# Turning the cached keys on VectorE during the FFNs, with a copy of them in HBM

## The reference

```
x = x + 0.5 * post1(SwiGLU_1(pre1(x)))      # 1024 -> 2816 -> 1024
z = pre_m(x) @ w_in                         # 2832 columns: GLA, stick-breaking attention, convolution
x = x + post_m(concat(groups) @ w_out)
x = x + 0.5 * post2(SwiGLU_2(pre2(x)))
```

```
past_k = cache_sb_k[l][page_table].reshape(DB, past_len, SB_HEADS, SB_DIM)
z = einsum('bqhd,bkhd->bhqk', q, k) * d**-0.5 + bias_h
A[t,s] = sigmoid(z_ts) * prod_{s<j<t} (1 - sigmoid(z_tj));   out = A @ v
```

## Time and profile before

| | |
|---|---|
| time, median of 3 runs | 1406.8 us (1406.1 to 1408.73) |
| span of the profiled execution | 1407.3 us |
| TensorE busy | 1391.1 us, 99% |
| VectorE busy | 899.6 us, 64% |
| ScalarE busy | 734.5 us, 52% |
| GpSimd busy | 182.6 us, 13% |
| HBM read, written | 242.10 MB, 5.53 MB |
| mean granted TensorE clock | 0.998 of full speed |

### The profile page before, as it was taken

The page is one execution under the profiler, slowest core; times in us unless marked ns, Lnnn a source line. Parts: engine busy times, 40 slices in busy tenths (PEclk is TensorE's granted clock), DMA queues, the critical chain, the costliest instruction groups (busy, mean ns, idle before and its releaser), DMA issues.

```text
span 1407.3 us, 26950 instructions
## 1 busy us (share of the span) xinstructions
PE 1391.1 (99%) x10551; PEld 1321.4 (94%) x10551; DVE 899.6 (64%) x1508; ACT 734.5 (52%) x1210; POOL 182.6 (13%) x333
## 2 busy tenths in 40 slices
PE   7999999999999999999999999999999999999998
PEld 6999999988878999999999999999888799999998
DVE  5666544669995876663367665346899858756542
ACT  4544434489766554443365444346887665444441
POOL 1020000323262110000000000021433510000000
PEclk9999999999999999999999999999999999999999
DMA  9575455577799595545545555564868895555541
GB/s 247 150 210 150 141 147 153 156 203 230 210 310 265 145 255 150 150 139 152 155 127 149 151 149 144 152 175 141 252 206 242 287 255 154 151 149 149 148 139 50
DMA packets 391554, 249.41 MB, mean 177 GB/s; under 512 B 16513, under 2 KB 379638, under 8 KB 391428
## 3 DMA queue, kind: packets, MB, share of 16 engines
q1 hardware_dynamic: 375602, 204.94, 51.2%
q0 software_dynamic: 15520, 42.62, 9.7%
q10 hardware_dynamic: 306, 0.13, 0.0%
HBM read 242.10 MB, written 5.53 MB: 176 GB/s over the span
## 4 chain that ended last, share of the span: by engine, by line
PE 94%; DVE 2%; ACT 1%; DMA 1%; issue 1%; SPq 0%; POOLq 0%; POOL 0%; DVEq 0%; ACTq 0%
PE bank L596 25%; PE bank L598 24%; PE bank L597 24%; PE bank L862 3%; PE bank L973 2%; PE bank L877 2%; PE bank L632 2%; PE bank L636 2%; PE bank L633 2%; PE bank L1050 1%; DMA raw<-in_ffn_w_gate 1%; PE bank L827 1%; PE bank L954 1%; PE bank L1168 1%; PE bank L1090 1%
## 5 line engine op out<-in xcount | busy, mean ns | idle before, releaser
L1602 DVE TENSOR_TENSOR w_l<-raw,w_h 128x1024 fp32r<-128x1024 f32 (+1 forms) x332 | 395.4, 1196 | 295.4 <-ACT w_h L1224 295.1
L596 PE MATMUL bank<-hh,w_h 128*128 128x320 f32 x1632 | 512.9, 314 | 0.0
L598 PE MATMUL bank<-hh,w_l 128*128 128x320 f32 x1632 | 504.4, 309 | 0.0
L597 PE MATMUL bank<-hl,w_h 128*128 128x320 f32 x1632 | 504.3, 309 | 0.0
L1224 ACT ACTIVATE w_h<-raw 128x1024 fp32r<-128x1024 f32 (+1 forms) x332 | 332.3, 1030 | 141.4 <-DMA raw<-in_ffn_w_down 101.4
L596 PEld LDWEIGHTS bank<-hh,w_h 128*128 128x128 f32 x1632 | 306.4, 188 | 11.8 <-issue 8.6
L597 PEld LDWEIGHTS bank<-hl,w_h 128*128 128x128 f32 x1632 | 306.5, 188 | 0.6
L598 PEld LDWEIGHTS bank<-hh,w_l 128*128 128x128 f32 x1632 | 306.4, 188 | 0.0
L596 PE MATMUL bank<-guh,w_h 128*128 128x320 f32 x704 | 217.7, 309 | 0.0
L598 PE MATMUL bank<-guh,w_l 128*128 128x320 f32 x704 | 217.4, 309 | 0.0
L597 PE MATMUL bank<-gul,w_h 128*128 128x320 f32 x704 | 217.4, 309 | 0.0
(11 more groups left out here) (297 smaller groups left out, 1604.9 us busy)
## 6 DMA issues: line engine op xcount, KB each, us to landing
raw<-in_ffn_w_gate SPq DMA_DIRECT2D x88, 512.0 KB, 4.0
raw<-in_ffn_w_up SPq DMA_DIRECT2D x88, 512.0 KB, 3.9
raw<-in_ffn_w_down SPq DMA_DIRECT2D x64, 448.0 KB, 3.8
raw<-in_w_in SPq DMA_DIRECT2D x44, 512.0 KB, 4.0
raw<-in_ffn_w_down SPq DMA_DIRECT2D x32, 512.0 KB, 4.0
kpg<-in_cache_sb_k SPq DMA_DIRECT2D x112, 128.0 KB, 3.3
kpg<-in_cache_sb_k POOLq DMA_DIRECT2D x112, 128.0 KB, 2.7
raw<-in_w_out SPq DMA_DIRECT2D x16, 512.0 KB, 6.9
```

The source lines that it names most:

```text
L596: pe.matmul(out, w_h[:, slot, k, :], rhs_h[:, k0 + k, :], start=first, stop=False)
L597: pe.matmul(out, w_h[:, slot, k, :], rhs_l[:, k0 + k, :], start=False, stop=False)
L598: last = pe.matmul(out, w_l[:, slot, k, :], rhs_h[:, k0 + k, :], start=False, stop=end)
L1602: V(dve.tensor_tensor(w_l[:, slot, 0:n, :], raw[:, slot, 0:n, :], w_h[:, slot, 0:n, :].bitcast(F32), ALU.subtract), sm["w_lo"])
```

## The change

- TensorE turns no keys any more, and ScalarE copies none. `kpz`, `kpg`, `turn_keys`, `turn_keys_early` and `copy_keys` are gone.
- A staged unit is the 4 pages of one batch in one step, 32 of them per layer. GpSimd loads the rows into `kn_` with 32 partitions for each quarter (`load_rows`, four DMAs of 128 KB), VectorE turns all 32x32 blocks by one instruction of 128x1024 into `kx_`, and GpSimd stores them to a new tensor `turned_keys` in HBM by four DMAs in pieces of 512 B (`store_turned`). Both buffers are double.
- VectorE's turns stand at fixed places in the FFNs: all 32 units of layer 0 in its first FFN (one a pair from the third pair on, then two for each of six output tiles); the 32 of layer 1 in the two FFNs between the mixers, 16 each.
- In the mixer SyncE alone loads a whole step from `turned_keys` (4 DMAs of 512 KB, 4 KB in one piece for each partition) to `kT`, double buffered by step. A score call covers a whole step, 512 columns, at the `m` of `SCORES_AT`, alternating between banks 4 and 2.
- GpSimd does its other work of the mixer (state loads, clearing buffers) after all stores of that layer's keys have landed (`all_stored`). The values of steps 0 and 1 are loaded when the score calls 6 and 7 are done.
- Some start-up semaphores are merged.

```diff
+SCORES_AT = {9: 0, 10: 1, 12: 2, 13: 3, 15: 4, 17: 5, 19: 6, 21: 7}
+SCORE_BANK = (4, 2)
...
+    turned_keys = nc.dram_tensor("turned_keys", [L, ITS, G, P, 2, 4, P], F32, kind="Internal").ap()
...
@@ SyncE
-                def keys(h):
...
-                        for j in range(2):
-                            sp_.dma_start(heads(kpg[l][:, h % 2, b, j, :]), page(sp_, ids[4 * b + 2 * (h % 2) + j], ins["cache_sb_k"], l)).then_inc(sm[f"ks_loaded{h % 2}"], 16)
+                def keys(it):
+
+                    for b in range(G):
+                        if it < 2:
                             sp_.wait_ge(sm["w_used"], U + U_IN + 4)
                         else:
+                            sp_.wait_ge(*at("kt_used", it - 1))
+                        sp_.wait_ge(sm[f"kx_stored{b % 2}"], 64 * (l * UNITS_K // 2 + 2 * it + b // 2 + 1))
+                        sp_.dma_start(kT[l][it % 2][:, b], turned_keys[l, it, b].rearrange("p a n s -> p a (n s)")).then_inc(sm[f"ks_loaded{it % 2}"], 16)
...
-                keys(2)
-                keys(3)
+                keys(0)
+                keys(1)
                 load_in(8)
                 load_in(9)
                 for m in range(7, 20):
                     load_in(m + 3)
-                    for h in range(4, 2 * ITS):
-                        if SLOT_OF[h - 2] == m:
-                            keys(h)
+                    for it in range(2, ITS):
+                        if SCORED[it - 2] == m:
+                            keys(it)
@@ GpSimd
+                def load_rows(i):
+
+                    g = l * UNITS_K + i
+                    if g >= 2:
+                        pool.wait_ge(sm["kx_turned"], g - 1)
+                    page_ids(pool, ids, i // G, (i % G,))
+                    for n in range(4):
+                        pool.dma_start(kn_[32 * n:32 * n + 32, g % 2], quarter(pool, ids[n], ins["cache_sb_k"], l)).then_inc(sm[f"kn_loaded{g % 2}"], 16)
+
+                def store_turned(i):
+
+                    g = l * UNITS_K + i
+                    pool.wait_ge(sm["kx_turned"], g + 1)
+                    for n in range(4):
+                        pool.dma_start(turned_keys[l, i // G, i % G, :, :, n, :].rearrange("(r p) a s -> p a r s", p=32),
+                                       kx_[32 * n:32 * n + 32, g % 2].rearrange("p (a r) s -> p a r s", a=2)).then_inc(sm[f"kx_stored{g % 2}"], 16)
...
                 else:
-                    pool.wait_ge(sm["w_used"], 16)
-                pool.wait_ge(sm["pages_loaded"], 32)
-                page_ids(pool, ids, 0, range(G))
-                for h in range(2):
-                    for b in range(G):
-                        for j in range(2):
-                            pool.dma_start(heads(kpz[:, h, b, j, :]), page(pool, ids[4 * b + 2 * h + j], ins["cache_sb_k"], l)).then_inc(sm["kz_loaded"], 16)
+                    pool.wait_ge(sm["w_used"], 8)
+                pool.wait_ge(sm["const_loaded"], 48)
+                load_rows(0)
+                load_rows(1)
+                for i in range(UNITS_K):
+                    store_turned(i)
+                    if i + 2 < UNITS_K:
+                        load_rows(i + 2)
+                all_stored(pool, l)
@@ TensorE
-                def turn_keys(h, batches):
...
+                def scores(it):
+
+                    pe.wait_ge(*at(f"ks_loaded{it % 2}", 64 * (it // 2 + 1)))
...
+                    if it >= 2:
+                        pe.wait_ge(*at("z_placed", it - 1))
+                    out = bank[SCORE_BANK[it % 2]]
                     for p_ in range(2):
                         for b in range(G):
                             c0 = (it // (PAGES // 4) * G + b) * 32
+                            last = pe.matmul(out[32 * b:32 * b + 32, :], qb[:, p_, c0:c0 + 32], kT[l][it % 2][:, b, p_, :],
                                              start=(p_ == 0), stop=(p_ == 1), skip_group_check=True)
@@ VectorE
+            def turn_keys(k2, units):
+
+                for _ in range(units):
+                    if staged[0] >= (1, 1.5, 2, 2)[k2] * UNITS_K:
+                        return
+                    g = staged[0]
+                    dve.wait_ge(sm[f"kn_loaded{g % 2}"], 64 * (g // 2 + 1))
+                    if g >= 2:
+                        dve.wait_ge(sm[f"kx_stored{g % 2}"], 64 * (g // 2))
+                    V(dve.transpose(kx_[:, g % 2].rearrange("p c (j s) -> p j c s", s=32), kn_[:, g % 2].rearrange("p j (c d) -> p j c d", d=32)), sm["kx_turned"])
+                    staged[0] += 1
...
                         V(dve.tensor_tensor(gul[:, 2 * i + t, :], gt[:, t, :], guh[:, 2 * i + t, :].bitcast(F32), ALU.subtract), sm["gu_lo"])
+                        if i and (k2 == 0 or t == 0):
+                            turn_keys(k2, 1)
...
                 for n in range(KD):
                     for m in range(3):
                         if 3 * n + m + LEAD < 3 * KD + 5:
                             lo(Ud + 3 * n + m + LEAD)
+                    if n < KD - 2:
+                        turn_keys(k2, 2 if k2 == 0 else 1)
```

More of the change, by code:

```diff
@@ L359, in page, with quarter, all_stored @@
         return cache[l:l + 1, bass.ds(eng.snap(reg, min_val=0, max_val=cache.shape[1] - 1), 1)].rearrange("l n p h d -> p (l n h) d")
+    def quarter(eng, reg, cache, l):
+        return cache[l:l + 1, bass.ds(eng.snap(reg, min_val=0, max_val=cache.shape[1] - 1), 1)].rearrange("l n (j p) h d -> p (l n j) (h d)", p=32)
+    def all_stored(eng, l):
+        for half in range(2):
+            eng.wait_ge(sm[f"kx_stored{half}"], 64 * (l + 1) * UNITS_K // 2)
     def heads(ap):
@@ L428, in values @@
                         for b in (0, 1):
[L429 to L432, removed]
+                            if it < 2:
+                                sp_.wait_ge(*at("kt_used", ITS - 1 + it))
                             else:
@@ L546, in store_rows @@
                     pool.dma_start(outs["sample_sb_" + name][l].rearrange("b t h d -> (b t) (h d)"), t[0:TS, 2, :]).then_inc(so, 16)
-                for h in range(2, 2 * ITS):
-                    keys(h)
-                    if h == 8:
+                for it in (4, 5, 6):
+                    if it == 4:
                         pool.wait_ge(*at("sk_placed", 2))
                         store_rows("k", skn)
-                    if h == 10:
+                    if it == 5:
                         pool.wait_ge(*at("cso_placed", 2))
@@ L1013, in _ @@
                         gate_rows(u, out, range(4))
-                    elif h == last_h:
+                    else:
                         unit(u, out, hh, hl, part=range(4))
-                    else:
-                        unit(u, out, hh, hl, part=range(3))
-                        turn_keys(h, (2, 3))
-                        unit(u, out, hh, hl, part=range(3, 5))
-                        turn_keys(last_h, (0, 1))
-                        unit(u, out, hh, hl, part=range(5, 6))
-                        scores(h)
-                        unit(u, out, hh, hl, part=range(6, 7))
-                    if last_h < 2 * ITS:
-                        turn_keys(last_h, (2, 3))
                     if m == 9:
@@ L1044, in _ @@
                     else:
-                        unit(u, out, hh, hl, part=range(4, KD) if h == last_h else range(7, KD))
+                        unit(u, out, hh, hl, part=range(4, KD))
                 def gla_outputs(pair):
@@ L1926, in _ @@
                         place_prompt(m - 13)
-                    for h in TURNS[m]:
-                        if h >= 2 and h % 2 == 0:
-                            log_weights(h // 2 - 1)
+                    if m in SCORES_AT:
+                        log_weights(SCORES_AT[m])
                     if m == NIN - 1:
```

186 lines of the change are left out of this document (51 added, 135 removed).

## The result

The changed kernel is slower: 1421.95 us (median of 4 runs, 1419.82 to 1423.58) against 1407.39 us, ratio 1.0102 with a 95% interval of 1.0087 to 1.0116. The forecast was 1410 us, a range of 1394 to 1428, and slower as the likeliest sign. Sign and range hold; the forecast is 12 us too small, and what follows is about those 12 us.

What follows compares the result with a forecast made beforehand. TensorE was busy 1391.1 of 1407.3 us, with VectorE nearly full too in the projection loop. A 15.6 us first-FFN loss minus a 12.6 us mixer gain gave +3.0 on the median 1406.8: about 1410 us, range 1394 to 1428.

Steps and rivals of the forecast that it cites:

- The 50.5 us: Two projection loops: TensorE's queue gets 50.5 us shorter, by 58 groups of eight key transposes at 0.87 us each.
- the upper bound: Projection loops: the gain is at most VectorE's idle time, 13.4 us in layer 0 and 11.3 in layer 1, together 24.7.
- the 12.6 taken: Mixers' gain: 4.9 us before layer 0's second log weights, 2.9 in layer 1, 4.8 in the long stretches after.
- Unit 9's split: Mixer's projection: keys ahead in SyncE's queue delay unit 9's weights, so its split starts near 287.6 us, not 283.81.
- the 1.6 us of first latency: Mixer, SyncE's queue: an estimated 1.6 us within the landing time of unit 9's weights, near 285.8 us.
- the rule that the prediction quotes: Mixer's key loads: starting DMAs from several engines saves only start time, so the single queue costs nothing; about 4 us more gain.
- The cycle where VectorE is behind: FFN gate loop: 5.58 us plus 1.15 for a transpose makes 6.73 us a pair, under TensorE's 7.04.
- Turn 19: Layer 0's first FFN: transpose 19 ends at 181.4 us, and GpSimd's work on the remaining units is counted from there.
- 11 U - 54.8: Layer 0's first FFN: loss in us, U being GpSimd's us per staged unit; 15.6 at U = 6.4.
- this sign of being wrong: Staging: the prediction is wrong if GpSimd's cost per unit is far from 6.4 us.
- The DMAs saturate: Rival, first FFN: U = 7.5 costs 27.7 us, net +15, 1422 us; chance 0.16.
- 149 + 217 GB/s wanted: First FFN's down projection: DMA rates wanted, set against 289 to 327 GB/s seen, as support for saturated DMAs.

Runs made afterwards that it cites:

- the taps: Changed kernel without six of the convolution's 31 taps, VectorE work in the projection loop: 1409.20 us; the kernel before without the same six: 1408.53 us.
- the other order in the queue: Changed kernel with SyncE issuing the loads of projection units 8 and 9 between the first and second four key loads, not behind both: 1425.31 us.

## Why the prediction held in sign and missed in size

**The gain.** TensorE's transposes left and VectorE became the bound: shown by the taps. The 50.5 us gave back 15.3, under the 24.7 of the upper bound and near the 12.6 taken. The steps can be followed in VectorE's log weights (line 1847 before, 1799 after). From the copy to the second of them: 57.1 us before (308.01 - 250.92), 52.55 after (330.36 - 277.81), 4.5 gained for 4.9 forecast; in layer 1 55.05 and 52.5, 2.5 for 2.9. From there to the last of them: 86.1 us before (394.11 - 308.01 in layer 0), 83.7 after (414.09 - 330.36), the same in layer 1, 2.4 gained for 2.4 forecast. The forecast ended there. The remaining 0.9 and 2.6 us were gained behind the loop, where it had nothing.

```profile
330.36 0.68 DVE L1799 SCALAR_TENSOR_TENSOR t__108<-z__107,t__108 128x512 f32<-128x512 f32 x1
...
414.09 0.68 DVE L1799 SCALAR_TENSOR_TENSOR t__108<-z__107,t__108 128x512 f32<-128x512 f32 x1
```

**The single queue.** Unit 9's split was forecast 3.8 us late and came 3.7 late (36.6 us after the copy; 32.9 before), though the 1.6 us of first latency in that sum had no row behind them. But the forecast booked this as lost gain, and with the other order in the queue nearly none of it came back: the next wait was as long. The event was right and its price wrong. That order was tried within one queue; two queues were not, so the rule that the prediction quotes from the Trainium skill, "DMA: Bandwidth & Descriptors", section "Issuing engines are not separate DMA queues", is neither shown nor refuted here.

**VectorE's transposes.** One takes 1.24 us, and 1.17 from its start to that of the next instruction (54.08 to 55.25); the forecast was 1.15 net. The cycle where VectorE is behind is 6.70 us (54.08 to 60.79), forecast 6.73. The Trainium skill, "Vector Engine (DVE) Microarchitecture Reference", section "The reshape front-end and per-opcode configuration", has one element per cycle and lane; the trace agrees with the estimate of 1.1 to 1.2 us that the prediction drew from it, 1.17 us net for 1024 elements a lane. But VectorE did not catch up: from the first to the twentieth turn it took (188.80 - 54.08)/19 = 7.09 us a pair, about TensorE's own pace, 7.4 us more in all than 19 cycles of 6.70. The 30.7 us for which its splits wait for ScalarE between 60 and 190 us are mostly not the reason: each pair has one such wait of 1.4 to 1.5 us inside the cycle (gate result, then ScalarE's `sg` and `w_h`, then the split), and it is in the 5.58 us of before too. What comes on top is 2.7 us of waits for rows and 4.2 us in three splits whose weights were late. Timelines of VectorE and ScalarE in the changed kernel:

```profile
57.18 1.22 DVE L1536 TENSOR_TENSOR w_l<-raw,w_h 128x1024 fp32r<-128x1024 f32 x1 [1.48 <-ACT w_h L1178]
...
136.07 1.06 ACT L1178 ACTIVATE w_h<-raw 128x1024 fp32r<-128x1024 f32 x1 [3.25 <-DMA raw<-in_ffn_w_up]
137.16 1.23 DVE L1536 TENSOR_TENSOR w_l<-raw,w_h 128x1024 fp32r<-128x1024 f32 x1 [2.16 <-ACT w_h L1178]
```

Turn 19 (the twentieth) ended at 190.0, forecast 181.4. With three tiles and an eighth of the stores neither wait is there behind the first turn, and it ended at 181.1: the forecast's count of VectorE was right for DMAs that come in time. TensorE waited 7.6 us for the last hidden tile, from 180.1, where the forecast had no stall before 241.

**The step that failed** is "A staged unit costs GpSimd four loads and four stores ... 6.4 us a unit", the U of 11 U - 54.8. The engine needs 2.43 us for four stores, 2.42 for four loads and some 0.2 between them where it is not held up, 5.05 us a unit, at which the formula gives a loss of 0.8. Timeline of GpSimd in the changed kernel:

```profile
103.31 2.43 POOL L508 DMA_DIRECT2D turned_keys<-kx__104  x4 [1.71 <-DVE kx__104 L1627]
105.89 2.42 POOL L501 DMA_DIRECT2D kn__103<-in_cache_sb_k  x4
```

A unit did cost more than 6.4, 6.75 us, but as the round of two tiles under full DMA engines. With 6.75 the formula gives 19.5; the turn 19 that starts it being 8.6 us late adds the rest, 28 for 26.9 measured. The prediction had named this sign of being wrong itself, a cost per unit far from 6.4 us. That it held in sign is luck in this part: with the 5.05 us that the engine needs, its own sum is 0.8 - 12.6 = -11.8, some 1395 us, faster. The rival "The DMAs saturate" was worked out as 27.7 us lost and 1422 us; it had the measured time and half of the cause, and only 0.16 of the chance, because GpSimd was thought too slow to fill the DMA engines. The line that spoke for it stood in the forecast itself: 149 + 217 GB/s wanted, 289 to 327 seen.

**Two limits in a row.** The taking away of one load or the adding of one tile gives back little by itself; both together give nearly all. With everything else equal:

| copy of the last tile, us | all bytes | an eighth of the stores |
|---|---|---|
| two tiles for rows | 277.8 | 272.2 |
| three tiles for rows | 273.9 | 253.7 |

Lifting one limit shows the other close behind it, at 272 to 274 us. Full DMA engines make the rows and weights land late: with three tiles and all bytes their share is still 1.11 from 190 us to the copy. And two tiles allow no more than two units on their way: with an eighth of the stores the share there is 0.95, and a unit still takes 6.3 us. In the FFNs that stage 16 units the share is 0.94 and 0.87 (from 486.8 to 724 and from there to 962 us), and staging costs 0.1 and 1.0 us.

Two cases are open. Two tiles with a quarter of the rows would tell whether DMA engines with room from the start need the third tile at all. And a third tile for the turned keys was not run, though the turn waits for a store for 13.0 us with three tiles for the rows.

## What to carry to other kernels

A wait that vanishes when a buffer is added is not yet time gained: look at the span and at what the engine waits for next, and lift two suspected limits together before ruling out either. Before moving bytes under another stage, add up the rate that each part of it will ask for and set it against the highest seen rate; the issuing engine's time is a second question. And where work is taken off one engine while another is 95% busy in the same loop, the gain is at most about the other's idle time (here 15.3 us of 24.7), not the work taken off (50.5).

## What was not expected of the hardware

- The rows weigh more than the stores. With three tiles, an eighth of the stores leaves the DMA engines full (share 1.14) at 241 GB/s and weights landing after 9.2 us; a quarter of the rows leaves room (0.92) at 254 GB/s and weights land after 5.4 us. The weights' own packets of 512 B show it: their queue's share by 16 x 110 us and by packets gives 28.0 ns each before, 36.6 in the changed kernel, 40.2 with an eighth of the stores, 28.8 with a quarter of the rows. So, with three tiles, it is the loading of rows that slows the loading of weights, and not the stores; why, no run here tells.
- GpSimd issues a store of 128 KB in 256 pieces (0.615 us) hardly slower than a load of 128 KB (0.553 us); the forecast took 0.80 and 0.65.
- Stalls are paid a second time in the clock: 20.8 us of standing still between 170 and 277.8 us came with 6.1 us more for the same matmuls, at a mean granted clock of 0.91 of full speed. In the mixers, where TensorE now waits for VectorE, the mean is 0.96 and 0.97 (1.00 and 0.99 before).
